# Key and value compression in attention: blocks stationary and weights streamed in 64x32 tiles, instead of weights stationary and blocks streamed

## The reference, cut to what matters

```python
def compress(kv, w1, w2, pe):            # kv: (1, 256, 2 groups, 64); used for keys and for values
    nc = (T - 32) // 16 + 1              # 15 blocks of 32 tokens, one every 16 tokens
    idx = arange(nc)[:, None] * 16 + arange(32)[None, :]
    blocks = kv[:, idx] + pe[None, None, :, None, :]
    blocks = swapaxes(blocks, 2, 3).reshape(B, nc, G, 32 * 64)
    return gelu(blocks @ w1) @ w2        # w1: (2048, 128), w2: (128, 64)
```

## Time and profile before

| what | value |
|---|---|
| runs | 1904.49, 1905.39, 1906.96 us |
| span of the profiled execution, first to last instruction | 1904.5 us |
| median of the runs less that span | 0.9 us |
| TensorE busy, share of the span | 1755.1 us, 92% |
| VectorE, ScalarE | 748.0 us (39%), 451.2 us (24%) |
| mean granted TensorE clock | 0.962 |
| attention's input side, from the first projection to the first score | 725 to 832 us |
| expert stage, from its first weight load | 895 us to the end |

### The profile page before, as it was taken

The page is one execution under the profiler, slowest core; times in us unless marked ns, Lnnn a source line. Parts: engine busy times, 40 slices in busy tenths (PEclk is TensorE's granted clock), DMA queues, the critical chain, the costliest instruction groups (busy, mean ns, idle before and its releaser), DMA issues.

```text
span 1904.5 us, 23817 instructions
## 1 busy us (share of the span) xinstructions
PE 1755.1 (92%) x9756; PEld 1111.8 (58%) x9756; DVE 748.0 (39%) x1141; ACT 451.2 (24%) x692; POOL 13.3 (1%) x20
## 2 busy tenths in 40 slices
PE   8999999999999999999999898888898888987986
PEld 5799889798479988966543334333343333423332
DVE  3655567675265553154323231222222222213236
ACT  1544456212054441134211101001010000101103
POOL 0000000000000000000000000000000000000000
PEclk9999999999999999899899899999999999988998
DMA  9544441200544443122899999999999999999993
GB/s 395 217 199 189 195 158 68 87 2 1 221 194 198 194 192 140 49 84 72 340 400 428 427 427 426 429 428 424 428 429 428 428 428 428 428 428 427 427 427 160
DMA packets 41329, 545.22 MB, mean 286 GB/s; under 512 B 4736, under 2 KB 4864, under 8 KB 8608
## 3 DMA queue, kind: packets, MB, share of 16 engines
q1 hardware_dynamic: 39088, 536.22, 67.4%
q0 software_dynamic: 1872, 6.82, 1.0%
q10 hardware_dynamic: 288, 1.05, 0.1%
HBM read 540.92 MB, written 3.15 MB: 286 GB/s over the span
## 4 chain that ended last, share of the span: by engine, by line
PE 75%; DMA 18%; DVE 3%; ACT 2%; issue 1%; SPq 0%; DVEq 0%; ACTq 0%
DMA ring<-experts_dram 18%; PE ps L536 6%; PE ps L2190 5%; PE ps L2167 5%; PE ps L2251 4%; PE ps L2212 4%; PE ps L651 3%; PE ps L650 3%; PE ps L649 3%; PE ps L725 3%; PE ps L723 3%; PE ps L724 3%; PE ps L1219 3%; PE ps L1437 2%; PE ps L2304 2%; PE ps L2238 2%
## 5 line engine op out<-in xcount | busy, mean ns | idle before, releaser
L778 DVE TENSOR_TENSOR ring_split<-ring,ring_split 128x1024 fp32r<-128x1024 f32 x156 | 187.2, 1223 | 128.8 <-ACT ring_split L830 128.8
L2190 PE MATMUL ps<-ring,arena 128*32 128x512 f32 x1152 | 159.5, 704 | 83.2 <-DMA ring<-experts_dram 83.1
L2684 DVE TENSOR_SCALAR arena<-ps 128x512 f32<-128x512 f32 (+1 forms) x38 | 21.5, 565 | 495.6 <-PE ps L2190 202.7
L830 ACT CAST ring_split<-ring 128x1024 fp32r<-128x1024 f32 x156 | 160.4, 1047 | 166.6 <-PE ps L725 92.0
L2212 PE MATMUL ps<-ring,arena 128*128 128x512 f32 x384 | 167.4, 594 | 0.2 <-DMA ring<-experts_dram 0.2
L2990 ACT ACTIVATE arena<-arena 128x512 f32<-128x512 f32 (+1 forms) x38 | 20.1, 530 | 575.7 <-DVE arena L2684 575.7
L2190 PEld LDWEIGHTS ps<-ring,arena 128*32 128x32 f32 x1152 | 41.5, 127 | 190.3 <-issue 184.5
L723 PE MATMUL ps<-arena_split,ring_split 128*128 128x256 f32 x512 | 145.4, 284 | 0.0
L725 PE MATMUL ps<-arena_split,ring_split 128*128 128x256 f32 x512 | 145.0, 283 | 0.0
L724 PE MATMUL ps<-arena_split,ring_split 128*128 128x256 f32 x512 | 144.5, 282 | 0.0
L2212 PEld LDWEIGHTS ps<-ring,arena 128*128 128x128 f32 x384 | 73.1, 191 | 88.4 <-issue 86.4
(11 more groups left out here) (438 smaller groups left out, 2532.6 us busy)
## 6 DMA issues: line engine op xcount, KB each, us to landing
ring<-experts_dram SPq DMA_DIRECT2D x192, 2048.0 KB, 20.0
ring<-weights_dram SPq DMA_DIRECT2D x55, 2048.0 KB, 11.6
row_buf<-rows_dram POOLq DMA_DIRECT2D x13, 512.0 KB, 10.0
ring<-weights_dram SPq DMA_DIRECT2D x3, 1024.0 KB, 11.0
tab<-tables_dram SPq DMA_DIRECT2D x1, 2160.5 KB, 31.8
tab<-weights_dram SPq DMA_DIRECT2D x1, 1536.0 KB, 25.7
gate_mid<-weights_dram SPq DMA_DIRECT2D x1, 1536.0 KB, 28.0
x<-tokens_dram SPq DMA_DIRECT2D x1, 1024.0 KB, 4.9
```

The lines of the kernel that those rows point to most:

```text
L778: V.tensor_tensor(low, raw, high, ALU.subtract).then_inc(sem("part_low"), 1)
L830: A.copy(split_buffer(MLP_SPLIT_SLOT, buffer)[0], raw).then_inc(sem("part_high"), 1)
L2190: ins = T.matmul(view(bank(0)[TINY * q:TINY * q + TINY], (2, 256)), xs_of(4 * c + d, j)[:, 0:TINY], w[q // 2][:, d, :, 256 * (q % 2):256 * ...
```

## The change

`pe_compress_first` swaps the operands. The stationary operand is now the block of position i, 64 partitions by 32 columns (30 columns and two of zeros), and the 64x128 weight block streams. The output of position i goes to the 32 partitions from 32*(i % 4), so that four positions and the two halves (keys in partitions 0 to 63, values in 64 to 127) use eight different 64x32 tiles of the array one after another. Each of the four partition groups gathers eight positions: `start` is set for the first four positions, `stop` for the last four. The result is four partial sums, each 32 blocks by 128 hidden columns, for keys and for values.

VectorE copies these out of PSUM (one instruction, 128x256), and `pe_compress_sum` makes two products of 128x128 by 128x32 with the table `own_expert`, which add the four groups and turn the result, so that the hidden columns are in the partitions again, beside the partial sums in the same banks. TensorE does this after the first quarter of the `kf` projection. `cmp_in` has 32 columns per position instead of 30, and one memset clears the two new ones; it carries the signal that the last addition carried before.

```diff
-        cmp_in = scratch(5696, 32, 30)
+        cmp_in = scratch(5696, 32, 32)
+        cmp_part = view(m_small[:, 0:256], (2, P))
...
             for r in range(4):
+                if r == 1:
+                    pe_compress_sum(pe)
                 m = turned(ps[:, 0, r * SEQ:(r + 1) * SEQ], w, 512, lambda a: a[:, r * P:(r + 1) * P])
...
-                    m = V.tensor_tensor(cmp_in[:, 16 * q:16 * q + 16, 15 * g:15 * g + 15], tokens_,
-                                        spread(pe_cols[:, 16 * q:16 * q + 16], 15), ALU.add)
-            m.then_inc(flag_up("cmp_in"), 1)
+                    V.tensor_tensor(cmp_in[:, 16 * q:16 * q + 16, 15 * g:15 * g + 15], tokens_,
+                                    spread(pe_cols[:, 16 * q:16 * q + 16], 15), ALU.add)
+            V.memset(cmp_in[:, :, 30:32], 0.0).then_inc(flag_up("cmp_in"), 1)
...
             V.tensor_copy(cumT, ps[0:8, 1, 512:768]).then_inc(sem("fox_cum"), 1)
+            v.wait_ge(*flag("cmp_part_psum"))
+            V.tensor_copy(cmp_part, view(ps[:, 3, :], (2, 512))[:, :, 0:P]).then_inc(flag_up("cmp_part"), 1)
             v.wait_ge(*flag("cmp_clear"))
             v.wait_ge(sem("cmp_hid"), 2)
...
             for i in range(32):
+                at = 32 * (i % 4)
                 for kv in range(2):
                     rows_ = slice(64 * kv, 64 * kv + 64)
-                    m = T.matmul(ps[:, 3, 512 * kv:512 * kv + 30], w[rows_, i * P:(i + 1) * P], cmp_in[rows_, i, :],
-                                 start=(i == 0), stop=(i == 31))
+                    m = T.matmul(ps[at:at + 32, 3, 512 * kv:512 * kv + P], cmp_in[rows_, i, :], w[rows_, i * P:(i + 1) * P],
+                                 start=i < 4, stop=i >= 28, skip_group_check=True)
+            m.then_inc(flag_up("cmp_part_psum"), 1)
+
+        def pe_compress_sum(pe):
+
+            pe.wait_ge(*flag("cmp_part"))
+            for kv in range(2):
+                m = T.matmul(ps[:, 3, 512 * kv + P:512 * kv + P + 32], cmp_part[:, kv, :], table("own_expert"), start=True, stop=True)
             m.then_inc(flag_up("cmp_hid_psum"), 1)
...
-                A.activation(hid[:, kv, :, 0:15], view(ps[:, 3, 512 * kv:512 * kv + 30], (2, 15)), ACT.Gelu_apprx_tanh)\
+                A.activation(hid[:, kv, :, 0:15], view(ps[:, 3, 512 * kv + P:512 * kv + P + 30], (2, 15)), ACT.Gelu_apprx_tanh)\
```

More of the change, by code:

```diff
@@ L46 @@
         "gdn_o1_psum", "att_kv_psum", "att_nat_psum", "att_qf_psum", "fox_cum_psum",
-        "cmp_hid_psum", "fox_rows1_psum", "cmp_kv_psum", "fox_rows0_psum", "cmp_score_psum", "cmp_pT_psum", "cmp_o_psum", "router_psum",
+        "cmp_part_psum", "cmp_hid_psum", "fox_rows1_psum", "cmp_kv_psum", "fox_rows0_psum", "cmp_score_psum", "cmp_pT_psum", "cmp_o_psum", "router_psum",
         "router_rank_psum", "router_wT_psum", "router_ids_psum", "router_sorted_psum",
@@ L52 @@
         "gdn_v_ready", "gdn_wT", "cmp_clear", "att_kv", "att_nat", "cmp_in", "fox_f", "fox_lf",
-        "cmp_hv4", "att_kf", "cmp_kcc", "cmp_vblk", "fox_bias", "cmp_diff", "cmp_prob", "cmp_pT", "cmp_o",
+        "cmp_part", "cmp_hv4", "att_kf", "cmp_kcc", "cmp_vblk", "fox_bias", "cmp_diff", "cmp_prob", "cmp_pT", "cmp_o",
         "router_top", "router_chosen", "router_rank", "router_weight", "router_perm", "router_wT", "router_ids",
```

## The result

The changed kernel takes 1895.89 us, the median of four runs (1893.61 to 1898.42), against 1905.04 us for the kernel before, also of four runs on the same chip: ratio 0.995, 95% interval 0.9936 to 0.9964. It was run again later (`after_again`): 1896.80 us against 1905.94 us, ratio 0.9953 (0.9937 to 0.9969). The forecast was 1896.2 us.

The account below looks back on a forecast made before the run. TensorE's chain was taken to bound the kernel up to the expert stage. Compression and kf go from 26.16 us to 2.4 + 13.92 + 0.6 = 16.9 us, a 9.2 us gain: 1896.2 us, range 1893.5 to 1901.3.

Parts of the forecast that it names:

- What bounds the kernel: TensorE's unbroken chain around the compression; expert transfers begin only when attention ends, so a gain passes on nearly one for one.
- The compression at 2.4 us: New product's 128 records, eight tiles abreast: 1.8 us, taken as 2.4 us for slower start and imperfect issue; before 10.76 us.
- The clock: In kf behind the compression: granted clock no longer falls, so kf takes 13.92 us instead of 15.40, gaining 1.48 us.
- The sum at 0.6 us: Four added sum-and-turn records after kf's first quarter: 0.6 us, between zero and 1.2 us, with VectorE's copy hidden.
- The fall behind the score products: Half clock slowing the value projection from 6.92 to 8.76 us; counted as staying, its 1.84 us can only be won.
- The gelu, the memset, the wider cmp_in: Side work around the compression: later gelu has nine us of cover, memset delays VectorE about 0.15 us; cost nothing.
- The 0.9 us around the span: Whole kernel: median of the runs stands 0.9 us above the profiled span, so 1895.3 us of span becomes 1896.2 us.
- Rival 1: Compression: record starts bind at 54 ns, product takes 6.9 us, clock stays up; gain 4.7 us, 1900.7 us; chance 0.14.
- Rival 2: Behind the compression: the clock falls in spite of the change; gain 7.5 us instead of 9.2, 1897.9 us; chance 0.10.
- Rival 3: Expert stage: bound by DMA, transfers meet something at a fixed time, gain not passed on; near 1905 us; chance 0.05.
- rival 4: Compression: tiles run one after another, product takes 25.4 us with the clock falling; slower, 1920.6 us; chance 0.03.
- The range of the forecast: Whole kernel: the forecast's own range, 1893.8 to 1897.5 us, its upper end from 3.6 us for the product; chance 0.68.

Follow-up runs that it names:

- e1: Changed kernel with each column tile given eight positions in a row, so only keys and values follow one another on different tiles; 1900.84 us, ratio to before 0.9978.
- e2: Changed kernel with all 32 positions of the keys first, then all of the values; 1897.71 us, ratio to the kernel before 0.9956.
- e3: Changed kernel with the 64 compression products issued four times in a row; 1909.06 us, ratio to the kernel before 1.0016.
- e7: Kernel before, its 64 old products dealt out in four parts of 16, each ahead of a quarter of kf; 1901.76 us, ratio 0.9973.
- e4: Changed kernel with the sum directly behind the compression instead of after the first quarter of kf; 1898.22 us, ratio to the kernel before 0.9954.
- e6: Changed kernel with the score products' loops reordered so the two key groups, in different row halves, take turns; 1891.76 us, ratio to the kernel before 0.9932.
- e8: Changed kernel with the 64 products issued three times, ahead of kf's first three quarters, and the sum ahead of the fourth; 1897.06 us, a single run.
- e5: Kernel before with only every second position in the compression, 64 old-form records in one piece; 4787 us, with four passes over the experts instead of one.

## Why the prediction was right, point by point

- *What bounds the kernel.* The chain of TensorE's work held, and the expert stage moved with the end of the attention. Right.
- *The compression at 2.4 us, between 1.8 and 3.6 us.* It took 1.96 us, with eight tiles abreast; e1 and e2 show that two and four abreast give 5.91 and 3.24 us. The allowance of 0.6 us for a slower start was 0.4 us too large. The 3.2 us of the rule that the prediction quotes, starts never closer than some 25 ns, did not come: they were 6 to 7 ns apart on different tiles, and 15 ns on average. The reason given for 1.8 us was incomplete, since a long series does not keep that pace: e3 took 25 ns a record over all (12.7 us for 512). The compression escapes that because it is only 64 calls with longer work around them; in e3 the record behind the first 256 starts 4.7 us after the first one, where two passes at 1.96 us would be 3.9 us. The prediction did not see this limit, and that the product stayed short of it was luck.
- *The clock, 1.48 us in kf and no fall.* Right: kf took 3.65 + 10.44 = 14.09 us against 13.92 us. The working did not set the clock apart within L1581 itself. By e7 the clock is worth 4.0 us even with eight changes of shape between (26.16 - 22.2), so at least four tenths of the gain are the clock's, and the other 5.8 us (22.2 - 16.41) are the tiles' less the sum, with fewer changes of shape in them; no run sets these apart.
- *The sum at 0.6 us.* It took 0.36 us on the chain, 0.53 us with kf's small surplus (16.41 - 1.96 - 13.92). That VectorE's copy costs nothing behind a quarter of kf was right, and its price without that cover is 0.6 us in e4, as the prediction said.
- *The fall behind the score products.* It stayed at its 1.84 us in the changed kernel. In e6 and in e1 it did not come, so it can be had, as the prediction said; what decides it is open.
- *The gelu, the memset, the wider cmp_in.* No wait of TensorE appears at any of them.
- *The 0.9 us around the span.* The profiled execution after shows a span 1.8 us under its own time (1893.2 and 1894.99 us), and so do all later ones. The 0.9 us of before thus mixed two executions: the profiled one was about 1 us slower than the median. It does no harm, since the forecast comes to the median less the gain. The gain of 9.2 us was 0.5 us too small by the chain (9.75 us); that it is nearer to the difference of the medians (9.15 us) is chance.
- *Rival 1 (starts bind)* did not come about: 15 ns a record and not 54. A long series is bound in e3, but at 25 ns. *Rival 2 (the clock falls in spite of it)* did not come about, and e3, where the clock did not fall in 12.8 us, speaks against it in general. *Rival 3* and *rival 4* did not come about.
- *The range of the forecast.* 3.6 us for the product give 1896.2 + 1.2 = 1897.4 us, where the prediction has 1897.5; nothing hangs on it.

## What to carry to other kernels

Small products that use part of the array should follow one another on different tiles: with 64x32 tiles the order of the loops alone moved the same instructions between 5.9 and 1.96 us, and in the score products between 3.25 and 1.89 us. Look at the granted clock beside each stretch of small products before its cost is written down, since the loss continues into the dense work behind it. And don't extend a rate from a short burst to a long series: four passes in a row took 12.7 us, and three passes with long calls between took 1.96 us each.

## What the runs showed of the hardware that was not expected

- A long series of short 32-bit products starts in bursts of 64 calls, each 2.03 us long, every 3.74 to 4.01 us, with one transfer of 16 KB of instructions to each burst (e3); among longer calls there is no pause (e8).
- A product in 64x32 tiles held the clock at 1.00 for 12.8 us although TensorE was idle for a third of it (e3), and so did the same product only two abreast for 5.9 us, with kf behind it at full speed (e1). The old form, a 64x128 load for 30 streamed columns, brought it to 0.50 after 3.4 us before and after 3.7 us in e5, but not in parts of 1.9 us (e7).
